# Second input projection: value tokens as split products of 512 columns, the indexer's key as one split piece with doubled columns

## The reference, cut to what matters

```python
DSA_W = MOBA_W = 4 * 128
IN_SIZES = (DSA_W, DSA_W, DSA_W, 8 * 64, 64, 8, MOBA_W, MOBA_W, MOBA_W, D_MODEL, D_MODEL)
h = rms_norm(x, g_mix_norm) * (1.0 + sc_m) + sh_m
proj = h @ w_in
(q_a, k_a, v_a, q_i, k_i, w_i, q_b, k_b, v_b, gate_a, gate_b) = jnp.split(proj, split_at, axis=-1)
# k_i: 64 columns, one key for all 8 indexer heads; w_i: 8 columns, a weight per head
logits = jnp.einsum('bqhd,bsd->bqhs', qi, ki)
score = jnp.einsum('bqh,bqhs->bqs', wi, relu(logits))   # picks 64 keys per query
# v_a, v_b: 512 columns each, the values of the two attentions
```

## Time and profile before

| what | value |
|---|---|
| time, median of 3 runs | 1595.24 us (1595.22 to 1598.74) |
| profiled execution, its own time | 1593.39 us |
| its span, first to last instruction | 1591.6 us |
| PE busy | 1331.5 us, 84% |
| DVE busy | 1024.8 us, 64% |
| ACT busy | 397.9 us, 25% |
| the changed stage, start of PE's first and last matmul | 1110.29 and 1230.63 us |
| mean granted clock of TensorE | 0.946 of full speed |

### The profile page before, as it was taken

How to read it: one execution, slowest core, us unless ns; L and a number is a source line. 1 busy time by engine, 2 the same in 40 slices (tenths; PEclk the granted TensorE clock), 3 DMA queues, 4 the chain that set the end, 5 groups by cost and what they waited for, 6 DMA issues and landing times. The chain is left out here.

```text
span 1591.6 us, 18182 instructions
## 1 busy us (share of the span) xinstructions
PE 1331.5 (84%) x6794; PEld 908.0 (57%) x6794; DVE 1024.8 (64%) x2382; ACT 397.9 (25%) x838; POOL 295.1 (19%) x297
## 2 busy tenths in 40 slices
PE   4986789998578888888888877776999787799988
PEld 2974377777433433333333322224897667799978
DVE  1696377774787878787878777666431677455442
ACT  3314300003411111111110101014333444544431
POOL 0003200000044444444344344430000000000000
PEclk8997898899789999999999999998999998899999
DMA  9455821127299999999999999996344106245543
GB/s 401 178 205 212 363 111 55 54 95 287 78 421 421 421 421 421 421 421 421 419 410 419 421 420 407 420 421 248 139 179 170 43 1 265 106 159 180 192 159 133
DMA packets 48184, 426.59 MB, mean 268 GB/s; under 512 B 5344, under 2 KB 5472, under 8 KB 5600
## 3 DMA queue, kind: packets, MB, share of 16 engines
q0 software_dynamic: 36864, 268.45, 40.7%
q1 hardware_dynamic: 11232, 156.98, 25.5%
HBM read 424.36 MB, written 1.05 MB: 267 GB/s over the span
## 5 line engine op out<-in xcount | busy, mean ns | idle before, releaser
L1277 PE MATMUL bank<-arena 128*128 128x512 f32 x1024 | 499.7, 616 | 128.5 <-DVE arena L1420 128.2
L1277 PEld LDWEIGHTS bank<-arena 128*128 128x128 f32 x1024 | 176.4, 190 | 436.8 <-DVE arena L1420 285.3
L1458 DVE CUSTOM_DVE_ANT_0 arena<-arena 128x1024 f32<-128x1024 f32 x256 | 313.6, 1225 | 148.8 <-DMA arena<-experts_in,arena 145.3
L1204 POOL DMA_INDIRECT arena<-experts_in,arena x256 | 274.2, 1071 | 605.9 <-PE bank L1277 352.8
L467 PE MATMUL bank<-rounded,rounded 128*128 128x256 f32 x1136 | 334.0, 294 | 44.6 <-DVE rounded L430 36.4
L469 PE MATMUL bank<-rounded,ring_r 128*128 128x256 f32 x1136 | 326.7, 288 | 0.0
L468 PE MATMUL bank<-rounded,rounded 128*128 128x256 f32 x1136 | 325.5, 287 | 0.0
L444 DVE TENSOR_TENSOR ring_r<-ring,rounded 128x1024 fp32r<-128x1024 f32 (+2 forms) x136 | 171.0, 1269 | 167.6 <-ACT rounded L439 167.5
L467 PEld LDWEIGHTS bank<-rounded,rounded 128*128 128x128 f32 x1136 | 221.8, 195 | 49.4 <-issue 28.4
L468 PEld LDWEIGHTS bank<-rounded,rounded 128*128 128x128 f32 x1136 | 223.0, 196 | 3.3 <-issue 3.3
L469 PEld LDWEIGHTS bank<-rounded,ring_r 128*128 128x128 f32 x1136 | 222.5, 196 | 0.0
(11 more groups left out here) (258 smaller groups left out, 1073.9 us busy)
## 6 DMA issues: line engine op xcount, KB each, us to landing
ring<-slots_in SPq DMA_DIRECT2D x73, 2048.0 KB, 8.4
arena<-experts_in,arena POOLq DMA_INDIRECT x256, 13.6
xT<-xT_in SPq DMA_DIRECT2D x1, 1024.0 KB, 11.0
mixT<-slots_in SPq DMA_DIRECT2D x1, 1024.0 KB, 7.1
out_dram<-xT SPq DMA_DIRECT2D x1, 1024.0 KB, 3.9
con<-consts_in SPq DMA_DIRECT2D x1, 552.0 KB, 9.0
vec<-vecs_in SPq DMA_DIRECT2D x1, 167.0 KB, 2.5
```

Source lines behind the costliest of these rows:

```text
L1204: pool.indirect_dma_start(rows[:, r % GRING, :], None, experts_in, bass.IndirectOffsetOnAxis(ap=expert[:, tt, at:at + 1], axis=0)).then_in ...
L1277: ins = pe.matmul(psum[2 * tt + half][:, :], diag[:, r % DIAGS, :], rows[:, r % GRING, D + 512 * half:D + 512 * half + 512], start=(h == 0 ...
L1458: dve.tensor_tensor_reduce(rows[:, r % GRING, 0:D], rows[:, r % GRING, 0:D], utok[:, tt, :], 1.0, 0.0, ALU.mult, ALU.add, hdot[:, r:r + 1] ...
```

## The change

The two tokens of a slot become split products. ACT casts the whole slot to a new area `whi` in two halves of 128 x 2048 elements (`act_token`), DVE subtracts in two halves and writes over the slot (`dve_token`), and PE multiplies with `xh` and `xl` as stationary operands and 512 moving columns, 24 matmuls per item. The key becomes one more "feat" piece: the host lays its 64 columns out twice, side by side, so that one piece of 128 columns gives both halves of the bank. The columns of the "weight" items move from 64 to 128 within slot 4. The stage has 29 pieces instead of 28, so a piece behind the key has an index one higher in `wi2`.

```diff
--- before.py
+++ after.py
@@ -1513,7 +1513,7 @@
         items += [item("feat", 1, i * P, qk[:, 4 + i, :]) for i in range(4)]
         items += [item("token", 2, tt, vtok[:, 0, tt, :]) for tt in range(TT)]
         items += [item("feat", 3, i * P, qki[:, i, :]) for i in range(4)]
-        items += [item("key", 4, 0, qki[:, 4, :])]
+        items += [item("feat", 4, 0, qki[:, 4, :])]
         items += [item("weight", 4, tt, wi[:, tt, :], scale=IDX_SCALE) for tt in range(TT)]
         items += [item("feat", 5, i * P, qk[:, 8 + i, :]) for i in range(4)]
         items += [item("feat", 6, i * P, qk[:, 12 + i, :]) for i in range(4)]
@@ -1522,6 +1522,20 @@
         i2_mm, i2_ev = sem("i2_mm"), sem("i2_ev")
         i2_feat = [n for n, it in enumerate(items) if it[0] == "feat"]
         wi2 = Split([(SLOTS["w_in2"][0] + items[n][1], 512, items[n][2], n) for n in i2_feat], KT, uT, 11552, i2_mm)
+        whi = area(21792, KT, CH, rounded=True)
+        tok_hi, tok_lo = sem("tok_hi"), sem("tok_lo")
+        TOKENS = (2, 7)
+
+        def act_token(act, s, half):
+            n, k = SLOTS["w_in2"][0] + s, slice(4 * half, 4 * half + 4)
+            wait_slot(act, n)
+            act.copy(whi[:, k, :], slot(n)[:, k, :]).then_inc(tok_hi, 1)
+
+        def dve_token(dve, s, half):
+            n, k = SLOTS["w_in2"][0] + s, slice(4 * half, 4 * half + 4)
+            dve.wait_ge(tok_hi, 2 * TOKENS.index(s) + half + 1)
+            dve.tensor_tensor(slot(n, rounded=True)[:, k, :], slot(n)[:, k, :], whi[:, k, :],
+                              ALU.subtract).then_inc(tok_lo, 1)
         with nc.Block() as block:
             @block.sync
             def _(sp):
@@ -1539,15 +1553,18 @@
                     if kind == "feat":
                         wi2.pe_products(pe, i2_feat.index(n), bank[:, 0:T]).then_inc(i2_mm, 1)
                         continue
-                    for half in range(2 if kind == "key" else 1):
-                        for k in range(KT):
-                            if kind == "key":
-                                o, l, r = bank[64 * half:64 * half + 64, 0:T], w[:, k, 0:64], uT[:, k, :]
-                            elif kind == "token":
-                                o, l, r = bank[:, :], uT[:, k, col * P:(col + 1) * P], w[:, k, :]
-                            else:
-                                o, l, r = bank[:, 0:HEADS], uT[:, k, col * P:(col + 1) * P], w[:, k, 64:64 + HEADS]
-                            ins = pe.matmul(o, l, r, start=(k == 0), stop=(k == KT - 1))
+                    cols = slice(col * P, (col + 1) * P)
+                    for k in range(KT):
+                        if kind == "weight":
+                            ins = pe.matmul(bank[:, 0:HEADS], uT[:, k, cols], w[:, k, P:P + HEADS],
+                                            start=(k == 0), stop=(k == KT - 1))
+                            continue
+                        if k % 4 == 0:
+                            pe.wait_ge(tok_lo, 2 * TOKENS.index(s) + k // 4 + 1)
+                        xh, xl = wi2.xh[:, k, cols], wi2.xl[:, k, cols]
+                        pe.matmul(bank[:, :], xh, whi[:, k, :], start=(k == 0), stop=False)
+                        pe.matmul(bank[:, :], xl, whi[:, k, :], start=False, stop=False)
+                        ins = pe.matmul(bank[:, :], xh, slot(s0 + s, rounded=True)[:, k, :], start=False, stop=(k == KT - 1))
                     ins.then_inc(i2_mm, 1)
 
             @block.scalar
@@ -1560,8 +1577,12 @@
                     act.wait_ge(i2_mm, n + 1)
                     if n == len(items) - 1 or items[n + 1][1] != s:
                         act.sem_inc(slot_used[(s0 + s) % RING], 1)
-                    width = {"feat": T, "key": T, "token": CH, "weight": HEADS}[kind]
+                    width = {"feat": T, "token": CH, "weight": HEADS}[kind]
                     act.activation(dst, psum[n % 8][:, 0:width], func, scale=scale).then_inc(i2_ev, 1)
+                    if n in (1, 3):
+                        act_token(act, 2, n // 2)
+                    if n in (19, 21):
+                        act_token(act, 7, (n - 19) // 2)
 
             @block.vector
             def _(dve):
@@ -1571,6 +1592,10 @@
                                              ALU.mult, ALU.mult)
                 for i in range(LEAD, len(i2_feat)):
                     wi2.dve_lo(dve, i)
+                    if i in (4, 6):
+                        dve_token(dve, 2, i // 6)
+                    if i in (18, 20):
+                        dve_token(dve, 7, i // 20)
         if STOP == "w_in2":
             return
 
@@ -1997,7 +2022,8 @@
     s = SLOTS["w_in2"][0]
     for j in range(4):
         tiles(s + j, wi[:, j * 512:(j + 1) * 512])
-    tiles(s + 4, np.concatenate([wi[:, 2048:2120], np.zeros((D, 440), np.float32)], axis=1))
+    tiles(s + 4, np.concatenate([wi[:, 2048:2112], wi[:, 2048:2120],
+                                        np.zeros((D, 376), np.float32)], axis=1))
     for j in range(5):
         tiles(s + 5 + j, wi[:, 2120 + j * 512:2120 + (j + 1) * 512])
     fill("gates", wi[:, 2120 + 5 * 512:])
```

## The result

| | us |
|---|---|
| before, median of 6 runs | 1596.05 (1594.75 to 1599.16) |
| changed, median of 6 runs | 1588.23 (1586.45 to 1590.76) |
| ratio | 0.9945, 95% interval 0.993 to 0.996 |
| profiled execution: span | 1587.7, against 1591.6 |

The account below looks back on a forecast made before the run. The prediction took PE alone to set the stage's pace. Gains of 6.72 us (tokens) and 3.42 (key) sum to 10.14, or 0.64% off the 1595.24 median: 1585.1 us, likely 1582.5 to 1588, range 1581 to 1590.5.

Parts of the forecast that it names:

- PE alone bounds the stage, and a gain reaches the end: PE busy every microsecond of the stage; later loads are released by compute, so a gain reaches the kernel's end undiminished.
- Token items: Two pairs on PE, 27.48 us before: 96 fp32r matmuls of 512 columns take 20.76 us, gain 6.72 (bounds 4.88 to 7.00).
- I take 216.3: Pace in ns for a 512-column fp32r token matmul, taken from float32 records of 256 columns; bounds 213.3 and 235.4.
- Rival 2: Token matmuls on PE: the load doesn't hide, 235.4 ns a matmul, gain 8.3 us, time 1587; chance 8%.
- Key: Key piece on PE: 6.25 us becomes 24 split matmuls of 117.7 ns, 2.83 us; gain 3.42.
- Weight items: Same count and shapes, so no gain; the clock's fall to 0.50 behind them, costing 1.2 us, left as it is.
- Rival 4: Clock: dips a fifth longer, or the one behind the weights takes two pieces more; 3 to 7 us lost, 1588 to 1592; 7%.
- ACT and DVE: Token halves: casts 1.9 us, subtractions 2.3 us each, costing nothing beside PE; pieces 5 and 7 early by 2.3 and 2.5 us.
- Loads: Slot 7's load and its first cast both move forward, but for the key's 3.4 us, leaving about 8.6 us.
- Sum: Whole stage: 6.72 from tokens plus 3.42 from the key, 10.14 us.
- Rival 3: PE waits for a `lo` behind a token subtraction on DVE, 1 to 4 us in all, time 1586 to 1589; 4%.
- Rivals 1 and 5: 512-column fp32r matmuls: 1, more than one column per cycle, time 1576, 2%; 5, half rate, 426.6 ns, time 1605, 4%.

Follow-up runs that it names:

- The cuts: Changed kernel, 512 columns of the token items cut differently: 111.7 ns at 128, 117.9 at 256, 175.7 at 384; 230.0 at 512 with 64 stationary columns.

## Why the prediction was right, and by how much it missed

- **The time.** The forecast was 1585.1 us, most likely from 1582.5 to 1588, in a range of 1581 to 1590.5. The first timing, 1588.23, lies in the range and just outside its core; the two later ones, 1585.82 and 1587.17, lie in the core. The timings alone can't tell the 8.6 us found below from the 10.1 forecast, since the first interval goes from 6.4 to 11.2.
- **PE alone bounds the stage, and a gain reaches the end.** Right, within about a microsecond. PE has no wait in the stage, and the stretch behind it is 360.4 to 364.4 us in four profiles of the changed kernel against 361.0 in the one of before.
- **Token items, the step that was mis-sized.** "I take 216.3" measured 232.3 ns, so the two pairs gain 5.18 us in place of 6.72. The mechanism, three runs over the columns for four, stands, and the value lies between my bounds, 213.3 and 235.4. What failed was the choice of the nearest row. I took float32 records of the same length and set aside the row of the same type, 117.7 ns at 256 columns, because I put its 11 ns down to a floor of 118 to 122 ns that would hide. The floor is 109 ns: the 122 had been read in a stretch at 0.92. Nor could the 213.3 ns at half clock show that a load hides there, since 8 columns take as long at that clock. The cuts show that the excess grows with the columns and little with the load. The stream of fp32r at full clock was the row to go by: twice 117.7 is 235.4, 1.3% off, and my value was 6.9% off. Rival 2 had the number nearly right, a gain of 8.3 us and 1587, and its reason, a load that doesn't hide, wrong for most of the excess.
- **Key.** 3.42 us, as worked out. Its gain is mostly in the doubled layout.
- **Weight items.** "I leave the dip as it is" holds roughly and in the mean only. Of four profiles of the changed kernel two have it, at 1.5 and 3.1 us, 1.2 in the mean of the four; the one of before had 1.6, of which the prediction counted the 1.2 behind the weights and not the 0.4 within them. Rival 4 isn't borne out: the longest dip is 1.5 us longer than that of before, and its smallest size was 3.
- **ACT and DVE.** 1.90 and 2.29 us, as interpolated. The slack was 1.7 and 2.5 us against 2.3 and 2.5 worked out, and the run with the longer work on DVE turned it into waits of nearly the size that follows from it.
- **Loads.** Right: no engine waited for a load in the stage.
- **Sum.** 8.60 us from the edit in place of 10.14. The three timings give 8.8, 9.9 and 8.5 us by their ratios. That the stage of the first profile, 109.27 us, is even shorter than the 110.2 that follow from the forecast is luck: the clock gave 2.4 us there that the prediction didn't count.
- **Rival 3** falls, since PE has no wait in the stage. **Rivals 1 and 5** fall with 1.09 cycles a column. The rule of the Trainium skill that rival 1 stood beside, "TensorE: Matmul & The Clock Gate", "Back-to-back issue gap", 131 ns for 512 columns, doesn't describe this stream; the isolated gap of that section, 216 ns, is 7% under the measured 232.3.

## What to carry to other kernels

Price a matmul by the row of its own type and let the number of columns change before the type does. Check the granted clock of a row before you take a floor from it. Here a float32 product that was already fed with 512 columns lost a quarter of its runs and about a fifth of its time by the split, with 1.9 us on ACT and 2.3 us on DVE per half slot, which both had to spare ahead of PE. Look for half-empty shapes first: doubling 64 stationary columns gave 2.8 us without any work on ACT or DVE, more than either token pair. And judge a change of a few microseconds by the length of its own stage in several profiles, since here the parts it didn't touch moved the span by 7 us.

## What the runs showed of the hardware

- From 256 moving columns up an fp32r matmul cost 0.447 ns for each further column at full clock, 1.07 cycles. At half clock one of 256 columns took 213.3 ns, no more than one cycle a column. Float32 records of 512 columns paid 1.006 cycles per run and column at full clock (429.4 ns for two runs). So the excess of fp32r at full clock didn't scale with the clock; what makes it is open. Loads beside it didn't change it (232.5 ns at a DMA share of 0.98, 232.7 at 0.00), and half the stationary columns took away 2.3 ns.
- A record has a floor that scales nearly with the clock: with 8 moving columns and 128 stationary ones it took 109 ns at full clock and 213.3 ns at half clock.
- A busy PE can be clocked down. While it was 100% busy with matmuls of 8 columns, the granted clock was 0.89 over the first 3.2 us and 0.50 over the 15 us of them that followed, in one execution. Where two groups of 1.7 us had 2.9 us of split matmuls between them, it stayed at 1.00 in three profiles.
